# Head norms of a two-layer attention and feed-forward kernel: means and factors with tokens on partitions, scaled rotation tables, and a projection group inside two norm stages

## What is computed

```python
def rmsnorm(x, g):
    xf = x.astype(jnp.float32)
    y = xf * lax.rsqrt(jnp.mean(xf * xf, axis=-1, keepdims=True) + EPS)
    return (y * g.astype(jnp.float32)).astype(x.dtype)

def rotate(x, cos, sin):
    x1, x2 = jnp.split(x, 2, axis=-1)
    return jnp.concatenate([x1 * cos - x2 * sin, x1 * sin + x2 * cos], axis=-1)
...
    # diff_attention: heads of 32; window_gqa and neighbourhood_attention: heads of 64
    x = rmsnorm(split_heads(x, 2 * DA_HEADS, DA_QK_DIM), gain)
    if rope:                      # DA and SW, latent tokens only
        x = apply_axial_rope(x, rope_tabs)
```

## Time and profile before

| | us |
|---|---|
| median of 3 executions | 2497.84 (2497.77 to 2499.87) |
| the profiled execution | 2500.59 |
| its span, first to last instruction | 2498.8 |
| mean granted TensorE clock | 0.901 |

### The profile page before, as it was taken

How to read it: one execution, slowest core, us unless ns; L and a number is a source line. 1 busy time by engine, 2 the same in 40 slices (tenths; PEclk the granted TensorE clock), 3 DMA queues, 4 the chain that set the end, 5 groups by cost and what they waited for, 6 DMA issues and landing times.

```text
span 2498.8 us, 29894 instructions
## 1 busy us (share of the span) xinstructions
PE 2085.4 (83%) x12484; PEld 1704.5 (68%) x12484; DVE 1168.2 (47%) x1782; ACT 767.3 (31%) x1225; POOL 606.8 (24%) x263
## 2 busy tenths in 40 slices
PE   5779795888673989999999978978788639899998
PEld 3657583666563768888888856757576536788887
DVE  2554547664787343131312244454865873522322
ACT  2423323334233142130312243232334332422321
POOL 0230010002453112222222213010001542334432
PEclk9889797898775989999999988979898869999999
DMA  7310010342231112122112213001033321233231
GB/s 263 59 52 18 17 35 15 104 133 79 68 102 34 34 34 68 53 66 68 61 58 68 68 35 76 18 18 34 18 107 79 118 68 51 68 102 98 88 101 68
DMA packets 178918, 168.86 MB, mean 68 GB/s; under 512 B 29200, under 2 KB 176096, under 8 KB 178656
## 3 DMA queue, kind: packets, MB, share of 16 engines
q1 hardware_dynamic: 176704, 161.18, 21.4%
q10 hardware_dynamic: 2080, 5.77, 0.8%
HBM read 159.07 MB, written 2.10 MB: 64 GB/s over the span
## 4 chain that ended last, share of the span: by engine, by line
PE 68%; DVE 16%; ACT 8%; issue 3%; POOL 2%; DMA 2%; ACTq 0%; SPq 0%; DVEq 0%; POOLq 0%
PE gp L723 53%; PE sp L856 3%; POOL HGx_kd L643 2%; PE gp L893 2%; PE tp L873 1%; PE sp L766 1%; PE sp L847 1%; ACT nt L1130 1%; PE sp L956 1%; PE gp L744 1%; ACT DA_p L1217 1%; PE op L873 1%; DVE sp L1486 1%; DVE sp L1485 1%; DVE HG_tmp L1799 1%
## 5 line engine op out<-in xcount | busy, mean ns | idle before, releaser
L667 POOL TENSOR_TENSOR wlo<-raw,whi 128x2048 fp32r<-128x2048 f32 x98 | 451.9, 4613 | 1654.4 <-ACT whi L1112 1654.2
L723 PE MATMUL gp<-xhi,whi 128*128 128x512 f32 (+1 forms) x1584 | 581.8, 367 | 97.9 <-DVE xlo L1506 52.1
L723 PE MATMUL gp<-xlo,whi 128*128 128x512 f32 (+1 forms) x1584 | 566.8, 358 | 0.0
L723 PE MATMUL gp<-xhi,wlo 128*128 128x512 f32 (+1 forms) x1584 | 564.9, 357 | 0.0
L723 PEld LDWEIGHTS gp<-xhi,whi 128*128 128x128 f32 x1584 | 308.8, 195 | 154.9 <-issue 52.7
L723 PEld LDWEIGHTS gp<-xhi,wlo 128*128 128x128 f32 x1584 | 308.0, 194 | 42.6
L723 PEld LDWEIGHTS gp<-xlo,whi 128*128 128x128 f32 x1584 | 308.6, 195 | 41.5 <-issue 1.7
L1112 ACT ACTIVATE whi<-raw 128x2048 fp32r<-128x2048 f32 x98 | 186.9, 1908 | 467.8 <-PE gp L723 443.5
L1867 DVE SCALAR_TENSOR_TENSOR xT<-gp,mods,xT 128x512 f32<-128x512 f32 x120 | 78.6, 661 | 476.1 <-PE gp L723 476.1
L723 PE MATMUL gp<-hhi,whi 128*128 128x512 f32 (+1 forms) x768 | 273.7, 356 | 9.3 <-ACT frel L1426 6.3
L723 PE MATMUL gp<-hlo,whi 128*128 128x512 f32 (+1 forms) x768 | 272.1, 354 | 0.0
(11 more groups left out here) (305 smaller groups left out, 2891.8 us busy)
## 6 DMA issues: line engine op xcount, KB each, us to landing
raw<-in_w_ff SPq DMA_DIRECT2D x64, 1024.0 KB, 5.3
raw<-in_w_mod SPq DMA_DIRECT2D x48, 1024.0 KB, 5.2
raw<-in_w_in SPq DMA_DIRECT2D x20, 1024.0 KB, 5.4
raw<-in_w_in SPq DMA_DIRECT2D x24, 256.0 KB, 4.6
raw<-in_w_out SPq DMA_DIRECT2D x8, 768.0 KB, 4.7
bias<-e SPq DMA_DIRECT2D x96, 32.0 KB
xin<-in_x ACTq DMA_DIRECT2D x1, 2048.0 KB, 9.4
raw<-in_w_out SPq DMA_DIRECT2D x16, 128.0 KB, 4.7
```

The source lines that it names most:

```text
L667: nc.gpsimd.tensor_tensor(wlo[:, s % 2, :, :], raw[:, index[splits[s]] % 2, :, :], whi[:, s % 2, :, :].bitcast(F32), ALU.subtract).then_in ...
L723: mm = pe.matmul(out, lhs, rhs, start=(i == 0 and j == 0), stop=(i == KT - 1 and j == 2))
```

## The change

All three norm stages are rewritten, and the constant tables lose one block of 128 unused columns.

1. **Means and factors with tokens on partitions.** The squares become the stationary side: for each block of 128 tokens one matmul against 2 (NA, SW) or 4 (DA) columns of the averaging matrix gives the means of all heads of the tile, tokens on partitions (`sums`). All tiles of a stage together are 36 to 96 columns of one bank. One Ln, one Exp and one Newton step (`factors`) serve the whole stage. ACT spreads each factor over its head's 32 or 64 columns (`wide`, a copy with a broadcast input), and PE transposes those blocks back into `sp` (`spread`), where DVE multiplies the tile by them (`scale`).
2. **Scaled tables.** In SW and DA the rotation works on the tile that is not scaled: DVE multiplies the permutation by the gain (`pg`), POOL the cosine table (`gc`), and the factor comes last, over the latent part by a plain product, over the context part together with the gain. POOL also multiplies tile by cosine table, and makes the low parts of tiles 0 and 1. The square of the last tile is DVE's.
3. **A dense group inside.** `fill_plan()` takes the first group of the next projection (`DAq` (0,0) in SW, `HGq` (0,0) in DA, 24 matmuls of 512 columns) out of `FILL[m, l]` and puts it into the norm stage: k-steps 0 to 3 before the transposes, 4 to 7 after them. The rest of the table is spread anew over the same units.
4. **NA.** PE makes the four groups of `NAv` with the transposes of the factors between them; DVE copies the value groups out between its scalings, not behind them.
5. **SW values.** The six value blocks go through `gp` in two lots (four, then two) with one copy each; the mask is copied as 256 columns and a zeroed block.

```diff
@@ fill_plan
+            if m in ("SW", "DA"):
+                u, c = chunks.pop(0)
+                plan[m + "n", l] = [[(u, c, 0, KT // 2)], [(u, c, KT // 2, KT)]]
@@ block.gpsimd
+            def head_norms(m, l):
...
+                pool.wait_ge(*upto(l, before + "_oread", pairs_of(before, l)))
+                wait_read(pool, ("prj", l, last_unit))
+                for k in range(2):
+                    ins = nc.gpsimd.tensor_scalar(gc[:, k, :], cf[:, cc:cc + LAT], gain_of(m, l, tiles[2 * k][0]), None, ALU.mult)
+                ins.then_inc(ls(l, m + "_pg"), 1)
+                pool.wait_ge(*upto(l, m + "_pg", 1))
+                for i, (n, ct, slot) in enumerate(tiles):
+                    pool.wait_ge(*upto(l, m + "_rot", i + 1))
...
+                    nc.gpsimd.tensor_tensor(x, x, gc[:, 1 if n[2] == "k" else 0, :], ALU.mult).then_inc(ls(l, m + "_cosd"), 1)
+                for i in range(2):
...
+                    pool.wait_ge(*upto(l, m + "_high", i + 1))
+                    nc.gpsimd.tensor_tensor(lo_parts[m][:, slot, 0:end], xr[:, slot, 0:end], hi_parts[m][i][:, 0:end].bitcast(F32),
+                                            ALU.subtract).then_inc(ls(l, m + "_lowp"), 1)
...
+                if u[0] == "prj" and u[2] in ("DAq", "HGq"):
+                    head_norms({"DAq": "SW", "HGq": "DA"}[u[2]], u[1])
@@ block.tensor
-                def average(i):
-                    pe.wait_ge(*upto(l, m + "_sq", i + 1))
-                    if i >= 2:
-                        pe.wait_ge(*upto(l, m + "_scaled", i - 1))
-                    for (a, b) in tile_segs(l, tiles[i][0]):
-                        mm = pe.matmul(sp_[:, 2 * (i % 2) + (1 if a else 0), 0:b - a], cf[:, AVG[m]:AVG[m] + P],
-                                       buf(m, "y")[:, i % 2, a:b], start=True, stop=True)
-                    mm.then_inc(ls(l, m + "_ms"), 1)
+                def sums(i):
...
+                    for b in range(blocks):
+                        mm = pe.matmul(sp_[:, 0, at + n * b:at + n * b + n], squared(m, i)[:, P * b:P * b + P],
+                                       cf[:, AVG[m]:AVG[m] + P:WIDE[m]], start=True, stop=True)
+                    mm.then_inc(ls(l, m + "_ms"), 1)
+                def spread(i):
+                    pe.wait_ge(*upto(l, m + "_wide", i + 1))
                     if i >= 2:
                         pe.wait_ge(*upto(l, m + "_scaled", i - 1))
...
+                    for b in range(end // P):
+                        mm = pe.transpose(spread_out(i, end)[:, P * b:P * b + P], buf(m, "y")[:, i % 2, P * b:P * b + P], ident)
+                    mm.then_inc(ls(l, m + "_rstd"), 1)
...
+                if m == "SW":
+                    pe.wait_ge(bank_free[0], dense_before[m, l])
+                    values(0)
+                turn(0)
+                turn(1)
+                sums(0)
+                sums(1)
+                if m == "DA":
+                    sums(3)
+                    turn(2)
+                sums(2)
+                turn(last_tile)
+                if m == "SW":
+                    values(1)
+                fill(FILL[m + "n", l][0])
+                for i in range(len(tiles)):
+                    spread(i)
+                fill(FILL[m + "n", l][1])
@@ block.scalar
+                def factors():
+                    at, n, blocks = head_cols(m, l, len(tiles) - 1)
+                    act.wait_ge(*upto(l, m + "_ms", len(tiles)))
+                    end = at + n * blocks
+                    link(nc.scalar.activation(rs[:, 0:end], sp_[:, 0, 0:end], ACT.Ln, bias=epsc[:, 0:1]))
+                    nc.scalar.activation(rs[:, 0:end], rs[:, 0:end], ACT.Exp, scale=-0.5).then_inc(ls(l, m + "_lnx"), 1)
+                def wide(i):
...
+                    nc.scalar.activation(buf(m, "y")[:, i % 2, 0:P * blocks].rearrange("p (b c) -> p b c", c=WIDE[m]),
+                                         rs[:, at:at + n * blocks].unsqueeze(2).to_broadcast([P, n * blocks, WIDE[m]]), ACT.Copy)\
+                      .then_inc(ls(l, m + "_wide"), 1)
@@ block.vector
                 def scale(i):
...
-                    link(refine(buf(m, "y")[:, i % 2, 0:end], averages(i % 2, end)))
...
+                    if m != "NA":
+                        a = LAT
+                        dve.wait_ge(*upto(l, m + "_roped", i + 1))
+                        ins = V.tensor_tensor(xr[:, slot, 0:a], xr[:, slot, 0:a], r[:, 0:a], ALU.mult)
+                    if a < end:
+                        ins = V.scalar_tensor_tensor(out=xr[:, slot, a:end], in0=xr[:, slot, a:end], scalar=gain,
+                                                     in1=r[:, a:end], op0=ALU.mult, op1=ALU.mult)
```

281 lines of the change are left out of this document (192 added, 89 removed).

## The result

| | before | after |
|---|---|---|
| median, us | 2497.84 (2497.77 to 2499.87) | 2426.88 (2425.44 to 2433.48) |
| profiled execution, us | 2500.59 | 2433.48 |
| its span, us | 2498.8 | 2431.7 |
| mean granted clock | 0.901 | 0.926 |

The ratio is 0.9746, with a 95% interval of 0.972 to 0.9772: 71 us faster, where 86 were forecast (2412). The profiled execution of either kernel is the slowest of its three; that of the changed one is 8 us above its fastest.

A forecast was written before the change was run, and what follows sets the result against it. PE was taken to bound the kernel (68% of the chain), with winnable time where it waits for DVE and ACT. Terms 44 + 14 + 17 + 11 = 86 us off 2500.6 gave 2414.6, against the median 2412; range 2394 to 2442.

The forecast's parts named there:

- four SW and DA stages: SW and DA norm stages of both layers: 19, 21.5, 16.5 and 19.5 us long, 44 us won.
- two NA stages: NA stages: PE's gaps of 12.20 and 5.70 us and the low-clock steps behind them go; 14 us won.
- the walk through the SW stage: SW stage of layer 0, priced instruction by instruction: 19 us instead of 29.6, 10.5 won.
- In the new order PE has no wait above 1 us: SW and DA stages: without such waits, the 9 us of low-clock work behind a stage should take 5.
- rival (b): SW and DA stages: means of few columns do not hold the clock; some 11 us lost per stage, 2456; chance 0.12.
- (d): SW and DA stages: slower than before if POOL's `gc` products take beyond 13 us each; chance 0.01.
- the tail collision: End of each SW and DA stage: DVE's low part waits for POOL's, priced at 1 us.
- Rival (a): SW and DA stages: POOL and DVE collide, 20 us less won, 2432; sign: additions of 2 us; chance 0.27 shared with another rival.
- The dense groups: Four groups of 24 steps leave the attentions: 5 us won in each SW, 3.5 in each DA, 17 in all.
- PE stands 28 of 155 us: DA attention: PE waits for softmax, so a moved dense group of 5.5 us wins only 3.5.
- The clock behind the stages: Start of the attentions behind SW and DA stages: less time at clock 0.50, 3 us each, 11 in all (0 to 16).
- no gap of PE above 2 us: NA stages: sign expected in the trace after the change, where gaps of 12.20 and 5.70 us stood before.

The follow-up runs named there:

- pad: Changed kernel with every SBUF buffer back at its address in the kernel before; 2419.47 us, ratio 0.9698.
- w_shift: Changed kernel with the factors' tile 128 columns wide: activation parts at their old address, weight parts still moved; 2408.79 us, ratio 0.9689.
- align256: Changed kernel with weight parts and activation parts both at multiples of 256 bytes; 2408.75 us, ratio 0.9677.
- before_shift: Kernel before with buffers at the changed kernel's addresses and the mask made by three instructions; 2508.51 us, ratio 1.0061.
- the spread half: Changed kernel with the first 12 dense steps of each SW and DA stage spread between the means; 2424.29 us, ratio 0.972.
- dve_all: Changed kernel with cosine products and low parts of the SW and DA stages on DVE, POOL keeping only `gc`; 2431.87 us, ratio 0.9741.
- dve_mix_w: Changed kernel with dense half between the means, activation parts at their old address, POOL's cosine products and low parts on DVE; 2415.64 us, ratio 0.9657.
- no_dense: Changed kernel with the four dense groups moved from the SW and DA stages back into the attentions; 2460.55 us, ratio 0.9857.
- mix_w: Changed kernel with the dense half spread between the means and activation parts at their old address; 2404.87 us, ratio 0.9634.

## Why the prediction was right, and where its size was off

The table sets the forecast beside the changed kernel's own profile, and beside the mean of the three profiles that have the change and a fast address (pad, w_shift, align256). All are differences to the profile of the kernel before, in us; boundaries are the first square of a stage, the DVE instruction that ends it, and the first instruction behind the DA attention.

| stretch | forecast | changed kernel | mean of three, fast address |
|---|---|---|---|
| four SW and DA stages | -44 | -35.9 | -39.8 |
| two NA stages | -14 | -13.2 | -10.6 |
| two SW attentions (dense 10, clock 6) | -16 | -8.9 | -10.4 |
| two DA attentions (dense 7, clock 5) | -12 | -21.5 | -23.7 |
| NA attentions, start | 0 | -0.8 | -3.4 |
| rest of layer 0, last stretch | 0 | +13.4 | -1.3 |
| sum | -86 | -66.9 | -89.2 |

**The time fell into the range, with one thing missing in the sum and two errors in it that cancel.** At the fast addresses the change gives 82, 93 and 93 us between spans, and 75, 78 and 81 by the ratios to the kernel before on the same chip; at the slow ones, from before_shift to the changed kernel, 75 between spans. The forecast was 86. So most of the 15 us that are missing in the changed kernel are the addresses, and on the fast side the total is within 11 of the forecast. That it comes so near is partly luck: against the mean of three, the stages and the SW attentions were put 4 and 6 us too high, the NA stages 3, and the DA attentions 12 too low.

The step that was never made: the prediction priced every instruction that the change adds or moves, and took all others at their old duration, among them 4512 dense steps of 512 columns. The diff shows both lines that moved their operands, the shorter table and the new tile. The last stretch has 1872 of these steps and got 11.8 us longer. In all, some 4100 spacings at clock 1.00 grew from 0.2278 to 0.2326 us, which makes 20 us, an estimate, if none of it hides behind a wait. In the rest of layer 0 the slower step is hardly seen in the changed kernel (+1.6 us there, with a clock of 0.93 instead of 0.91), and I can't say from these runs how much of it is hidden behind waits.

**The four stages: right mechanism, 4 to 8 us too much.** Three steps of the walk through the SW stage were off. "In the new order PE has no wait above 1 us" was right up to the last dense step (then 1.82 us in SW and 1.14 in DA of layer 0), and the conclusion that the clock stays high was wrong: it fell in the middle of the means with PE busy. That is rival (b), at a third of its price, since only the third tile's means, one permutation and the first steps of the dense half ran low, about 3.2 us, not 8.6. In layer 1 the spread half kept it from falling each time; in layer 0 it did not, and align256 had no fall in the SW stage without it. So the order counts, and it does not decide alone. Second, `gc` took 1.56 to 1.64 us, once 2.43, and not 1.2. Here are the changed kernel's instances by source line:

```profile
L728 POOL TENSOR_SCALAR SWn_gc<-cf,gq x2: 1642/2036/2429, 229.0 to 1573.5; 128x512 f32<-128x512 f32 x2
L728 POOL TENSOR_SCALAR SWn_gc<-cf,pcol x2: 1559/1560/1562, 230.6 to 1575.9; 128x512 f32<-128x512 f32 x2
```

The range of the prediction, half to twice 1.25, holds them; (d) needed 13 each. Nobody waited on the path for them: the means ended later. Third, the tail collision was priced at 1 us a stage and cost 1.4 in SW of layer 0 (2.40 against 0.96), 0.9 in DA (1.84) and next to nothing in layer 1 (low parts of 1.01 and 0.95).

**Rival (a) was seen and cost nothing that these runs can tell.** Additions of 1.67 us, its own sign, did occur, four times in the trace; the stages of dve_all and dve_mix_w, without them, are not shorter in sum.

**The dense groups: 17 forecast, more measured.** The no_dense kernel is 21 us slower in the median. In SW the 5 us each hold (4.6 and 6.4). In DA the term that was mis-sized is "PE stands 28 of 155 us, waiting for softmax steps that get no shorter; between 0 and 5.5, I take 3.5". Layer 1 shows it best: by the boundaries of the table that attention lasts 113.6 to 114.0 us in the three profiles with the group in it (the kernel before, before_shift, no_dense) and 101.2 to 103.6 in the eleven without, at least 10 us apart, where the group has 5.5 us of steps. PE's busy time is 92 to 93 us against 82 to 84, and the granted clock 0.87 to 0.89 against 0.91 to 0.94. In layer 0 the profile of the kernel before flatters the change: its DA attention lasts 154.6 us at clock 0.84, that of before_shift, the same work, 148.4 at 0.88, and no_dense 151.6 at 0.87, against 139 to 145 in the others. So of the 21.5 us of the table a few are variation of the kernel before. Part of what comes on top of the steps goes with the higher clock; what brings it about is not settled. Idle time in an attention is no proof, then, that moved work wins nothing.

**The clock behind the stages: 11 forecast, its place was wrong.** After the SW stage of layer 0 the clock was at 0.50 from 250.7 to 260.7, nearly as long as it had been before (until about 282 for a stage that ended at 270.6). PE had stood from 248.0 to 249.8, and then again for softmax. In SW nothing of the 6 us is seen (the attentions gained 5.1 and 3.8, the dense group's price); in DA it can't be told from the dense group's share.

**NA stages: 14 forecast, 10.6 to 13.2.** The gaps of 12.20 and 5.70 are gone, but the sign "no gap of PE above 2 us" failed in layer 0, in every profile that has the change (2.05 to 3.2 us). In the changed kernel:

```profile
145.46 0.66 PE L917 MATMUL tp<-cf,NA_vt 128*128 128x128 f32 x2 [2.97 <-DVE NA_vt L1724]
```

The last value copy waits behind a low part that took 3.43 us beside POOL. Part of the gain was given back, too: in layer 1 the clock now falls at the value transposes and in the first 12 us of the attention (its stretch is 69.5 us in the changed kernel, 66.8 before; in w_shift, align256 and mix_w, where it did not fall there, about 65), and a low part can still be caught by POOL's 5 us instruction, as pad shows with 4.98 us of PE's wait.

## What to carry to other kernels

When a diff changes the size or place of any buffer, price the work that reads the buffers behind it too, or keep their addresses; look at the spacing of one long run of equal matmuls before and after, since it takes one look and shows a slower pace that no wait and no clock shows. When many matmuls of a few columns stand in a row, read the granted clock inside the row, and try a few wide ones between them; here it helped in two stages of four. Before a difference between two single profiles is put down to a change, look at the same stretch in a second execution of either kernel.

## What the runs showed of the hardware

- **The address of the moving operand sets the pace of float32r steps of 512 columns.** The mean spacing at granted clock 1.00 is 0.2267 to 0.2268 us in the last 300 us of the profiles (0.2277 to 0.2278 over all of them) at two addresses of the activation parts, 0 and 160 bytes above a multiple of 256. It is 0.2324 to 0.2333 (0.2326 to 0.2332) at two others, 32 and 96 above; seven profiles against seven. 64 bytes make no half-way value. Steps of 256 columns do not follow: 0.1194 to 0.1196 at the first two, 0.1189 to 0.1190 at 32 above, 0.115 at 96 above. Four addresses don't make a rule; why is open, and whether the low parts or the high parts count was not tried, since all moved together.
- **The clock fell with PE busy all the time.** In the changed kernel 10 to 18 means of 2 or 4 columns had started when it fell from 1.00 to 0.50. With three dense steps behind each tile's means it stayed at 1.00 in the stages of layer 1, four profiles of four; in layer 0 it fell with them too, and once, in align256, it did not fall in the SW stage without them. The Trainium skill ("TensorE: Matmul & The Clock Gate", "Part 1") has the clock fall after idleness; by that rule alone the stretch 233.60 to 240.10, with no idle time, would have been at 1.00.
- **DVE's low part waits for a whole POOL instruction that started before it:** 5.28 us beside POOL's, which had started 0.8 us earlier, in pad, and 2.27 for two of them in the changed kernel's profile, where that instruction of POOL started 4 us after the first of them, with the same order of instructions. That is some 4 us in PE's wait behind them (4.98 against 0.94); dve_mix_w has the long form again (5.27). The Trainium skill ("SBUF — State Buffer", "Who interferes with whom") has the exclusion, and both rows agree with it.
- **POOL's product of 128 x 512 float32 with a per-partition scalar takes 1.56 to 1.65 us** (2.42 or 2.43 for the first one of the SW stage of layer 1), the product of two tensors of that size mostly 1.26 to 1.29.
